# Two modulation units between the layers, turns in 32x32 blocks, and one reciprocal for four heads

## What is computed

```python
# modulation: six vectors of 1024 per layer, for the latent tokens (c) and for the context (c_ctx)
sh1, sc1, g1, sh2, sc2, g2 = split(silu(c) @ w_ada + b_ada)          # w_ada: 1024 x 6144
h = rms_norm(x, norm1_g) * (1 + sc1) + sh1
# one projection of h feeds latent attention, a convolution, differential attention and three gates
o_diff = rms_norm(diff_attend(...), diff_subln_g) * (1 - lam_init)    # norm over the 128 channels of each of 4 heads
y = sigmoid(gate0) * (o_mla @ w_o_mla) + sigmoid(gate1) * (o_conv @ w_o_conv) + sigmoid(gate2) * (o_diff @ w_o_diff)
x = x + g1 * (y @ w_out)
h2 = rms_norm(x, norm2_g) * (1 + sc2) + sh2
x = x + g2 * hier_moe(h2)                                             # 32 experts, two per token
```

## Time and profile before

| | us |
|---|---|
| median of 3 runs | 1632.97 |
| lowest, highest | 1632.71, 1634.61 |
| the profiled execution | 1632.14 |
| its span, first to last instruction | 1630.1 |

### The profile page before, as it was taken

One profiled execution on the slowest core, in us unless ns is written; L12 is line 12 of the kernel. 1 busy time (PEld: TensorE's weight loads), 2 busy tenths in 40 slices (PEclk: granted clock), 3 DMA queues, 4 the chain that ended last, 5 costly groups with the idle time before them and its releaser, 6 DMA issues.

```text
span 1630.1 us, 18983 instructions
## 1 busy us (share of the span) xinstructions
PE 1494.2 (92%) x7490; PEld 823.2 (50%) x7490; DVE 635.5 (39%) x1416; ACT 385.9 (24%) x881; POOL 180.2 (11%) x144
## 2 busy tenths in 40 slices
PE   6999999999999999989988879999989998998874
PEld 4444444444444445655544457645757767443331
DVE  2468924433244303523111156972433314432223
ACT  4012313422223012212211142403522212110001
POOL 0001410000001110012211100240000100111110
PEclk9999999999999999999999989999999999999997
DMA  9323331112222234489999965542142456999995
GB/s 386 155 104 149 141 151 55 53 52 103 104 104 103 113 143 169 156 315 417 418 419 421 382 267 206 228 166 103 52 155 104 168 206 266 408 419 420 419 360 185
DMA packets 53099, 356.53 MB, mean 219 GB/s; under 512 B 10226, under 2 KB 10738, under 8 KB 21392
## 3 DMA queue, kind: packets, MB, share of 16 engines
q1 hardware_dynamic: 43920, 339.51, 51.8%
q0 software_dynamic: 8224, 12.61, 2.1%
q10 hardware_dynamic: 864, 3.15, 0.5%
HBM read 351.29 MB, written 19.14 MB: 227 GB/s over the span
## 4 chain that ended last, share of the span: by engine, by line
PE 73%; DMA 13%; DVE 6%; SPq 4%; ACT 2%; issue 1%; POOLq 0%; DVEq 0%; ACTq 0%
PE bank L337 69%; DMA arena<-w_up_in 11%; ACT arena L911 2%; SPq L2044 2%; PE bank L624 2%; DVE arena L1278 2%; DVE arena L1617 1%; PE bank L806 1%; DMA arena<-glu_in 1%; SPq L2061 1%; SPq L2052 1%; PE bank L411 1%; DMA arena<-ada_in 1%; PE bank L822 0%; DMA x<-x_in 0%
## 5 line engine op out<-in xcount | busy, mean ns | idle before, releaser
L337 PE MATMUL bank<-arena 128*128 128x512 f32 (+9 forms) x5464 | 1265.0, 462 | 64.8 <-DMA arena<-w_up_in 47.4
L337 PEld LDWEIGHTS bank<-arena 128*128 128x128 f32 (+3 forms) x5464 | 629.0, 158 | 581.0 <-issue 387.2
L911 ACT ACTIVATE arena<-bank 128x512 f32<-128x512 f32 (+6 forms) x502 | 218.9, 463 | 1042.8 <-PE bank L337 917.0
L1278 DVE SCALAR_TENSOR_TENSOR arena<-arena,bank 64x256 f32<-64x256 f32 (+3 forms) x121 | 57.7, 477 | 482.2 <-ACT arena L911 292.7
L1278 DVE SCALAR_TENSOR_TENSOR arena<-arena,vec 128x512 f32<-128x512 f32 (+1 forms) x262 | 182.6, 765 | 0.7
L1536 DVE TENSOR_REDUCE am<-bank 128x1 f32<-128x512 f32 (+1 forms) x96 | 55.5, 599 | 170.5 <-PE bank L337 170.5
L1950 POOL DMA_INDIRECT y<-arena,routing x65 | 62.7, 964 | 380.6 <-DVE arena L1815 191.3
L1927 POOL TENSOR_TENSOR arena<-arena 128x512 f32<-128x512 f32 (+1 forms) x32 | 31.9, 996 | 583.7 <-DVE arena L1278 583.7
L911 ACT ACTIVATE arena<-bank,am 128x512 f32<-128x512 f32 (+1 forms) x96 | 58.6, 613 | 78.4 <-DVE am L1539 78.3
L337 PE MATMUL bank<-arena,silz 128*32 128x512 f32 x384 | 46.3, 600 | 1.9 <-ACT arena L911 1.6
L624 PEld LDWEIGHTS bank<-con,arena 128*128 128x128 f32 x240 | 29.4, 142 | 36.4 <-issue 23.6
(11 more groups left out here) (154 smaller groups left out, 732.8 us busy)
## 6 DMA issues: line engine op xcount, KB each, us to landing
arena<-w_down_in SPq DMA_DIRECT2D x65, 1024.0 KB, 24.1
arena<-w_gate_in SPq DMA_DIRECT2D x61, 1024.0 KB, 21.8
arena<-w_up_in SPq DMA_DIRECT2D x61, 1024.0 KB, 28.7
arena<-ada_in SPq DMA_DIRECT2D x24, 2048.0 KB, 8.1
arena<-mg_in SPq DMA_DIRECT2D x12, 2048.0 KB, 7.8
arena<-mo_in SPq DMA_DIRECT2D x6, 2048.0 KB, 10.4
arena<-glu_in SPq DMA_DIRECT2D x4, 2048.0 KB, 11.7
arena<-out_w_in SPq DMA_DIRECT2D x4, 2048.0 KB, 15.1
```

Source lines behind the costliest of these rows:

```text
L337: return nc.tensor.matmul(out, w, rhs, start=start, stop=stop)
L911: return nc.scalar.activation(out, in_, fn, **kw)
L1278: return V.scalar_tensor_tensor(out, in0, sc, in1, op0=op0, op1=op1)
```

## The change

It does three things.

1. **Two units between the layers.** `("ada", 1, 4)` and `("ada", 1, 5)` come behind the last unit of layer 0 (`between`). SP issues their loads behind the overflow block's w_down, after `gu_full` 31. TensorE computes them after the last expert block: the first unit, the spread of g2, its turn, the second unit, its turn. ScalarE copies the first ahead of g2's rows and the second behind them. VectorE evacuates both behind `scales(1, 0)` and ahead of the first `mixed`. Layer 1 then has the units 6 to 11 left, behind glu0, lora, glu1, dq, ukv and dk; nothing stands behind dv and mo0.
2. **Turns in 32x32 blocks.** `ada_turn` has `pick` (128x32) as weights and streams the copied block, 128 columns at a time, into four groups of 32 rows of a bank. VectorE then transposes the bank's 128x128 in blocks of 32x32 into `whats`, waits for itself, and adds the bias. The columns of `w_ada` are permuted on the host to fit.
3. **One reciprocal.** The four sums have 32-column weights of ones and fill four groups of rows of one bank. One root, one reciprocal. Four matmuls with a single row of ones each then spread the rows of the reciprocal over 128 partitions of four "d" banks, from which VectorE multiplies `qd`. While the reciprocal is made, TensorE does gates 1 and 2 (in layer 1 also 3); behind the four spreading matmuls it does one gate more, 3 (in layer 1: 4), and then the first branch projection.

```diff
--- before.py
+++ after.py
@@ -278,22 +278,24 @@
                     del more[:1]
             if l == 0:
                 units_of_0 = len(units)
+                units += more[:2]
+                del more[:2]
         assert not more
         unit_no = {u: i for i, u in enumerate(units)}
-        first_of_layer1 = unit_no[("glu", 1, 0)]
+        between = (units_of_0, units_of_0 + 1)
         ring_of = [[(n_ - 3 + i_) % NRING for i_ in range(3)] for n_ in (units_of_0, len(units))]
 
         def ada_behind(key):
             n = 0 if key is None else unit_no[key] + 1
             out_ = []
-            while n < len(units) and units[n][0] == "ada":
+            while n < len(units) and units[n][0] == "ada" and n not in between:
                 out_.append(n)
                 n += 1
             return out_
 
         def ada_tmp(n):
             before = [k_[0] for k_ in units[:n] if k_[0] != "ada"]
-            if not before or before[-1] in ("lora", "glu"):
+            if n in between or not before or before[-1] in ("lora", "glu"):
                 return ka[:, n % 4, :]
             return PT[:, 1, :] if before[-1] in ("dq", "ukv", "dk", "dv") else lora[:, 2, :]
 
@@ -370,8 +372,7 @@
                 ps = begin("d", ("adaT", la, u))
                 pe.wait_ge(empty["a"], number["a"][("ada", la, u)])
                 for m in range(4):
-                    last = mm(ps[:, 2 * m:2 * m + 2], ada_tmp(n)[:, 128 * m:128 * m + 128],
-                              con_at("pick")[:, 0:2], True, True)
+                    last = mm(ps[32 * m:32 * m + 32, 0:128], con_at("pick"), ada_tmp(n)[:, 128 * m:128 * m + 128], True, True)
                 end("d", last)
 
             def ada_finish(key):
@@ -676,17 +677,27 @@
                 for k in range(KD):
                     gate_step(2, 0, k)
                 pe.wait_ge(s["exp_ready"], len(AU) + 2 * len(DU))
+                pe.wait_ge(s["stat_ready"], 1 + HD)
+                ps = begin("a", ("dn", l))
                 for i in range(HD):
-                    pe.wait_ge(s["stat_ready"], 2 + i)
-                    sums(("dn", l, i), [P[:, i, q0:T]])
-                for c in (1, 2):
+                    last = mm(ps[32 * i:32 * i + 32, 0:T - q0], ones[:, 0:32], P[:, i, q0:T], True, True)
+                end("a", last)
+                for c in (1, 2) if l == 0 else (1, 2, 3):
                     for k in range(KD):
                         gate_step(2, c, k)
+
+                pe.wait_ge(s["recip_ready"], 2)
+                for i in range(HD):
+                    ps = begin("d", ("dnb", l, i))
+                    end("d", mm(ps[:, 0:T - q0], ones[32 * i:32 * i + 1, :], P[32 * i:32 * i + 1, 0, q0:T], True, True))
                 ada_finish(("mo1", l, 0))
-
-                pe.wait_ge(s["recip_ready"], 1 + HD)
+                for c in (3,) if l == 0 else (4,):
+                    for k in range(KD):
+                        gate_step(2, c, k)
+
+                pe.wait_ge(empty["d"], number["d"][("dnb", l, HD - 1)])
                 for c in range(KD):
-                    if c >= 3:
+                    if c >= (4 if l == 0 else 5):
                         for k in range(KD):
                             gate_step(2, c, k)
                     for k in range(4):
@@ -896,7 +907,11 @@
                 pe.wait_ge(s["y_act"], NB[l])
                 pools.update(WIDE)
                 if l == 0:
+                    ada_unit(units[between[0]])
                     spread_rows(l, "g2", ada[l], 5 * KD, TOK)
+                    ada_turn(between[0])
+                    ada_unit(units[between[1]])
+                    ada_turn(between[1])
 
 
 
@@ -1159,9 +1174,8 @@
                 for i in range(HD):
                     f(P[:, i, q0:T], qd[:, i, q0:T], ACT.Square).then_inc(s["stat_ready"], 1)
                 gate(2, 0)
-                for i in range(HD):
-                    ps = take(("dn", l, i))
-                    give(f(P[:, i, q0:T], ps[:, 0:NQ], ACT.Sqrt, scale=1.0 / (2 * DH), bias=eps))
+                ps = take(("dn", l))
+                give(f(P[:, 0, q0:T], ps[:, 0:NQ], ACT.Sqrt, scale=1.0 / (2 * DH), bias=eps))
                 for c in range(1, KD):
                     gate(2, c)
                 ada_raw(("mg5", l, 0))
@@ -1253,7 +1267,9 @@
                                 extra(j)
 
                 if l == 0:
+                    raw_copy(between[0])
                     row_copies(l, "g2", TOK)
+                    raw_copy(between[1])
                 f(small[:, 13:14], small[:, 13:14], ACT.Sqrt)
 
             for q, t in ((6, 2), (7, 3)):
@@ -1291,7 +1307,9 @@
             def ada_evac(key):
                 _, la, u = key
                 ps = take(("adaT", la, u))
-                give(V.tensor_tensor(ada[la][:, 4 * u:4 * u + 4, :], grid(ps[:, 0:8], 4),
+                turned = whats[:, 128 * (u % 2):128 * (u % 2) + 128]
+                step(V.transpose(turned, ps[:, 0:128]))
+                give(V.tensor_tensor(ada[la][:, 4 * u:4 * u + 4, :], grid(turned, 4)[:, :, 0:2],
                                      vec_at(la, "b_ada")[:, 4 * u:4 * u + 4].unsqueeze(2).to_broadcast([128, 4, 2]), op=ADD))
 
             def scales(l, which):
@@ -1612,10 +1630,11 @@
                     merge_tiles(nA + u)
                 out_d(len(DU) - 1)
 
+                dve.wait_ge(empty["a"], A[("dn", l)])
+                V.reciprocal(P[:, 0, q0:T], P[:, 0, q0:T]).then_inc(s["recip_ready"], 1)
                 for i in range(HD):
-                    dve.wait_ge(empty["a"], A[("dn", l, i)])
-                    step(V.reciprocal(P[:, i, q0:T], P[:, i, q0:T]))
-                    stt(qd[:, i, q0:T], qd[:, i, q0:T], vec_at(l, "sub_g"), P[:, i, q0:T]).then_inc(s["recip_ready"], 1)
+                    ps = take(("dnb", l, i))
+                    give(stt(qd[:, i, q0:T], qd[:, i, q0:T], vec_at(l, "sub_g"), ps[:, 0:NQ]))
                 ada_finish(("mo1", l, 0))
 
                 scales(l, 2)
@@ -1852,6 +1871,8 @@
 
                 if l == 0:
                     scales(1, 0)
+                    for n in between:
+                        ada_evac(units[n])
                     mixed(0, 2, 0)
                     mixed(0, 3, 1, lambda: row_rstd(S[1], 0))
                     row_half(S[1], 0, 2)
@@ -2018,7 +2039,7 @@
                 s = S[l]
                 nx_d = 4 if l == 0 else 2
                 gu, wd = slot_places(ring_of[l])
-                while n < len(units) and (l == 1 or n < first_of_layer1):
+                while n < len(units) and (l == 1 or n < units_of_0):
                     load(n)
                     n += 1
                     if n == 1:
@@ -2101,6 +2122,10 @@
                     gate_, up_, down_ = block_loads(0)
                     expert_quarters(2, [gate_, up_], quarter_ready[0])
                     sp.dma_start(*down_).then_inc(wd_ready[2], 16)
+                    sp.wait_ge(s["gu_full"], 31)
+                    for _ in between:
+                        load(n)
+                        n += 1
                 nx = sp.value_load(meta[l][0:1, 15:16], min_val=0, max_val=OVER)
                 with sp.If(nx > X0):
                     sp.wait_ge(s["gu_full"], NE if X0 else 27)
@@ -2207,7 +2232,7 @@
         "final_g": A(final_g).reshape(1, D),
         "x": np.concatenate([A(ctx)[0], A(x)[0]], 0).reshape(4, 128, D).transpose(1, 0, 2),
         "router": np.concatenate([rows(w_rg, KD), rows(w_re, KD)], 3),
-        "ada": flat(rows(w_ada, KD).reshape(L, 128, KD, NADA, 512).transpose(0, 3, 1, 2, 4), 3),
+        "ada": flat(rows(w_ada, KD).reshape(L, 128, KD, NADA, 4, 4, 32).transpose(0, 3, 1, 2, 5, 4, 6), 3),
         "lora": flat(win[:, None, :, :, 0:LW], 3),
         "glu": flat(glu.transpose(0, 4, 1, 2, 5, 3, 6), 3),
         "dq": flat(win[:, None, :, :, o_q:o_k], 3),
```

## The result

| | before | changed |
|---|---|---|
| median of the runs on one chip, us | 1634.61 (5 runs, 1632.71 to 1635.97) | 1621.17 (5 runs, 1617.15 to 1625.14) |
| the profiled execution, us | 1632.14 | 1625.14 |
| its span, us | 1630.1 | 1623.3 |

The ratio is 0.9919, with a 95% interval of 0.9904 to 0.9934: 13.2 us faster, between 10.8 and 15.7. The profiled execution of the changed kernel is the slowest of its five.

A forecast was written before the change was run, and what follows sets the result against it. TensorE was 73% of the chain, DMA 13%, with a DMA-bound stretch between layers. Turns 6.0 + 0.5, norm 2.9 + 3.1, units 3.1 + 2.5, gap -2.2 save 15.9: 1632.14 to 1616.2, median 0.8 above, 1617.1; range 1612 to 1624.

The forecast's parts named there:

- Turns, 6.5 forecast: TensorE's turns fall from 0.81 to 0.41 us: 6.0 saved within matmul streams, 0.5 for six outside.
- Norm of layer 1, 3.1 forecast: Layer 1's attention norm, sums through broadcasts, falls from 11.28 to 8.1 us, saving 3.1.
- Norm of layer 0, 2.9 forecast: Layer 0's attention norm, sums through moved gate, falls from 19.17 to 16.25 us, saving 2.9.
- then the turn, 0.43: In layer 0's norm, a turn follows the four broadcasts on TensorE and takes 0.43 us.
- Units out of layer 1, 3.1 + 2.5 forecast: Layer 1's emptied places save 3.1 us behind dv and 2.5 behind mo0.
- The gap, 2.2 forecast: Between the layers, the two moved units make layer 1 start 2.2 us later, bounds 0 and 6.
- since the loads end about when it would end, I take 2.0: Between the layers, the last scatter of y lands 2.0 us later beside the two loads, out of 0 to 3.5.
- between about 939 and 948.8 SP's queue is empty: Between the layers, ten microseconds of DMA time are free for the two 2 MB loads.
- 953 with the slowest DMA engine: Between the layers, the second unit lands at 953, the case behind the upper bound of 6 us.
- the gap costs 6: Rival: between the layers 6 us are lost instead of 2.2, slowest DMA engine and VectorE's order, total 1621; chance 0.12.
- VectorE's tie: Ahead of layer 1, evacuation and first sum over y are both due at 955.7, so 0.2 us is added.
- The last scatter landing within 5 us: Sign to look for in the profile after: between the layers, the last y scatter lands within 5 us.

The follow-up runs named there:

- n_order: The changed kernel without the moved units, layer 0's turn behind mo1 put behind the third gate's matmuls: 1619.23 us, ratio 0.991 to before.
- p3_norm: The kernel of before with only the norm changed, old turns and no moved units: 1629.69 us, ratio 0.9981.
- p23_turns_norm: The kernel of before with turns and norm changed, the units staying in layer 1: 1620.36 us, ratio 0.9923.
- two_late_order: The changed kernel, both moved units later on the engines, layer 0's turn behind mo1 put behind the third gate: 1619.82 us, ratio 0.9925 to before.
- g_split: The changed kernel with each of the two loads between the layers issued as four of 1024 columns: 1619.91 us, ratio 0.9907 to before.

## Why the prediction was right, and where not

The sign and the range held: 1621.17 lies within 1612 to 1624. The forecast of 1617.1 went by a median of before of 1632.97 and saved 15.9 us; measured are 13.2, and 15.7 is the end of the interval, so the saving was set a little too high. Of the 4.1 us between forecast and time 1.6 come from before itself, which is at 1634.61 in these runs. By its steps:

- **Turns, 6.5 forecast.** A turn takes 0.43 us, forecast 0.41. Its eight records start in two groups of four, 0.13 us apart: the four column groups run at once with 128 columns as they do with 512. The kernel with the turns alone gave 7.9 (interval 5.2 to 10.5), its trace 6.3. Right. The Trainium skill, "TensorEngine Tiling (Array Packing)" (Key Properties), says that a change of tiling mode drains TensorE; a whole turn of 0.43 us, both changes included, bounds what that costs here.
- **Norm of layer 1, 3.1 forecast:** 2.96. Both waits of the earlier trace rows are gone, sums 0.64 and broadcasts 0.71, forecast 0.62 each. Right.
- **Norm of layer 0, 2.9 forecast:** 1.93 where the clock stays up. The failed step is "then the turn, 0.43": I let it follow the broadcasts at once, and did not count banks. The four broadcasts fill all four, and the turn waits 0.82 us for VectorE's first product. n_order removes that wait. The other 0.2 are the gates, 13.93 for my 13.7. In six of eight traces the lower clock takes 1.7 us more (more in p3_norm), which no step of mine had.
- **Units out of layer 1, 3.1 + 2.5 forecast.** Behind dv: 149.28 without the moved units, 146.22 with them, 3.06. Behind mo0: 161.83 to 159.37 in the kernel with the units alone, 2.46. Right; attention begins 0.69 us behind the last dv product.
- **The gap, 2.2 forecast, bounds 0 and 6:** 5.1 and 5.2. This is the term that was mis-sized. The failed step is "since the loads end about when it would end, I take 2.0", with its base "between about 939 and 948.8 SP's queue is empty". The 939 is where w_up lands; w_down was issued behind it at 928.7, and the trace of before has it landing 13.0 us later, at 941.7. The 949 to 951 for the end of the loads took all 16 engines to end together. In the changed kernel the last part of the second load lands at 948.60, which is 953.6 on before's clock (the last up matmul comes 4.95 us earlier now). That is the "953 with the slowest DMA engine" of my own upper bound, and the rival "the gap costs 6" is what happened, though by half of its mechanism: the loads of y wait for the scatter, and the scatter lands with that last part. It takes 7.19 us instead of the 2.3 of p23_turns_norm, 4.9 more. VectorE's tie, for which I added 0.2, costs 0.7: the first sum comes 5.6 us behind y's loads, 4.85 when its queue is free (two_late_order). Another 0.7 comes back later, where layer 1's weights had been late by as much.
- **The marks I named.** "The last scatter landing within 5 us" failed at 7.2; "y's loads 5 us later would make it wrong" came true in its relative sense: they come 14.1 us behind the last up matmul, 9.2 before (in absolute time 948.78 and 948.82, because layer 0 ends 5 us sooner). "No idle time ahead of the first branch" holds; the wait moved ahead of the turn.

The rule that I had cited, "DMA: Bandwidth & Descriptors" of the Trainium skill (Queues, rings and completion order), says that an engine takes turns between its queue rows packet by packet, and drains a whole packet, typically 9 to 17 descriptors, before it switches. What I drew from it, that the scatter is held up only while the two loads last, is what the traces show; what failed was the time at which the loads end. How far the packets take turns these runs don't settle, since none shows how large a packet of the loads is: with whole loads the scatter's last part lands 0.16 us behind theirs, with loads in quarters (g_split) 0.6 us ahead of theirs (947.68 and 948.32).

With the measured terms the sum is 6.3 + 1.9 + 3.0 + 3.1 + 2.5 - 5.1 = 11.7 us, inside the interval of 10.8 to 15.7. The moved units sum to 5.6 - 5.1 and measure as nothing; what the change brings, the turns and the norm bring.

A version that keeps what pays (turns, norm, one unit moved and placed late) ran at 0.9897 and 0.9905 of before, beside 0.9923 for the changed kernel on the same chip: 2.3 and 3.1 us better by the medians, with intervals that still touch.

## What to carry to other kernels

An idle stretch of DMA time is not free if a small transfer that everything waits for goes through it. Fill it only with what has landed, in its last part, by the time that transfer would land, and count from the last part of what is already queued, not from when most of it is through. Here 2 MB fitted (by 0.6 us) and 4 MB didn't (by some 5 us). When a transfer must come first, look next at the engine that works in order: an evacuation put in front of the sum that waits for the transfer held that sum up by 2.7 us for one unit, and moved behind it by nothing. And count banks when several results are put in a row ahead of something unrelated.

## What the runs showed of the hardware

- Eight records with 32-column weights and 128 streamed columns in four column groups take 0.43 us, changes of form included; four broadcasts from single rows 32 apart (8 records, 1x512) take 1.14 us and with 256 columns 0.71, where one by one they would take 3.4 and 1.7 (0.43 and 0.21 a record). Four row groups run at once, too.
- Turning a tile of 128x128 in 32x32 blocks, out of a bank, takes VectorE 0.32 us.
- Two loads of 2 MB behind a full queue end unevenly: of the second one's 16 parts ten landed by 942.74 and six from 945.21 to 948.60, and the queue ahead of them was as uneven (w_down: ten by 932.76, the last at 938.19). With rows of 4 KB instead of 16 KB the last part landed at 948.32.
- A small scatter on another queue, issued at 941.59 while the loads were under way, landed 0.16 us behind their last part, 7.2 us after its issue.
- TensorE's granted clock falls to half (1.2 of 2.4 GHz) for 3 to 4 us (7 in p3_norm) in stretches where TensorE is busy nearly all the time, at other places in other traces of the same kernel, and a fall of 3 to 4 us costs 1.7 us. The timelines of the first and the second trace of the changed kernel show it, the same eight matmuls, each time 0.3 us behind a wait of 2.0 us, in 4.89 and in 3.19 us:

```profile
283.04 0.44 PE L625 MATMUL bank<-con,arena 128*128 128x128 f32 x2 [2.01 <-DVE arena L1569]
283.31 4.89 PE L339 MATMUL bank<-arena 96*128 96x256 f32 x8
```

```profile
283.55 0.44 PE L625 MATMUL bank<-con,arena 128*128 128x128 f32 x2 [2.02 <-DVE arena L1569]
283.82 3.19 PE L339 MATMUL bank<-arena 96*128 96x256 f32 x8
```

The Trainium skill, "TensorE: Matmul & The Clock Gate" (Part 1), says that the gate goes by how busy TensorE has lately been and looks at moments of its own, so that one kernel is caught differently from run to run. The two traces agree with that. It sets a floor to what a single pair of traces can tell: stages have to be compared with the falls in them counted out.
